# RWKV scan: odd pairs of heads change sides of the partitions at each step of the triangular inverse

## What is computed

```
def step(S, inp):
    r_t, w_t, k_t, v_t, a_t, b_t = inp
    sa = einsum('bhvk,bhk->bhv', S, a_t)
    S = S * w_t[:, :, None, :] + sa[..., None] * b_t[:, :, None, :] + v_t[..., None] * k_t[:, :, None, :]
    return S, einsum('bhvk,bhk->bhv', S, r_t)
```

## Time and profile before

| what | us |
|---|---|
| median of 3 runs | 1949.92 |
| runs | 1946.99 to 1952.98 |
| the profiled execution | 1955.08 |
| its span | 1953.3 |
| TensorE busy in the span | 1862.2 |
| VectorE busy | 1290.7 |
| ScalarE busy | 1026.4 |
| scan, first L2753 to the first matmul after it (L413) | 152.06 |

### The profile page before, as it was taken

How to read it: one execution, slowest core, us unless ns; L and a number is a source line. 1 busy time by engine, 2 the same in 40 slices (tenths; PEclk the granted TensorE clock), 3 DMA queues, 4 the chain that set the end, 5 groups by cost and what they waited for, 6 DMA issues and landing times.

```text
span 1953.3 us, 46364 instructions
## 1 busy us (share of the span) xinstructions
PE 1862.2 (95%) x17956; PEld 1782.7 (91%) x17956; DVE 1290.7 (66%) x2627; ACT 1026.4 (53%) x2027; POOL 45.2 (2%) x38
## 2 busy tenths in 40 slices
PE   6999989999988999999999999999989978999998
PEld 6999989999988999989899999999976878899998
DVE  5778676778675665586566664766476755557764
ACT  5556646556645555555465554655445733245553
POOL 2110001110000000000000000000000000000000
PEclk9999999999998999999999999999989979989999
DMA  7444555445553555532235555555541500035654
GB/s 259 153 150 154 158 168 164 147 148 158 152 183 108 182 173 173 167 105 89 64 111 160 174 173 179 162 172 172 182 164 56 152 12 4 4 92 179 185 183 127
DMA packets 75675, 278.05 MB, mean 142 GB/s; under 512 B 8336, under 2 KB 9744, under 8 KB 75024
## 3 DMA queue, kind: packets, MB, share of 16 engines
q1 hardware_dynamic: 75536, 276.04, 45.5%
HBM read 274.96 MB, written 1.05 MB: 141 GB/s over the span
## 4 chain that ended last, share of the span: by engine, by line
PE 81%; DVE 10%; ACT 5%; issue 2%; DMA 1%; DVEq 0%; SPq 0%; ACTq 0%
PE psum L413 23%; PE psum L415 22%; PE psum L414 22%; DVE weights_low L378 4%; ACT weights_high L370 2%; PE psum L2835 1%; PE psum L2818 1%; PE psum L2832 1%; PE psum L1900 1%; PE psum L2776 1%; PE psum L2535 1%; PE psum L2753 1%; PE psum L718 1%; PE psum L1145 1%; PE psum L739 1%
## 5 line engine op out<-in xcount | busy, mean ns | idle before, releaser
L378 DVE TENSOR_TENSOR weights_low<-weight_ring,weights_high 128x512 fp32r<-128x512 f32 x988 | 669.7, 697 | 482.5 <-ACT weights_high L370 472.8
L370 ACT ACTIVATE weights_high<-weight_ring 128x512 fp32r<-128x512 f32 x988 | 608.4, 628 | 552.6 <-PE psum L415 547.4
L413 PE MATMUL psum<-ffn_normed_high,weights_high 128*128 128x272 f32 (+1 forms) x1408 | 407.4, 289 | 7.9 <-DVE ffn_normed_low L646 5.2
L415 PE MATMUL psum<-ffn_normed_high,weights_low 128*128 128x272 f32 (+1 forms) x1408 | 405.7, 288 | 0.0
L414 PE MATMUL psum<-ffn_normed_low,weights_high 128*128 128x272 f32 (+1 forms) x1408 | 404.4, 287 | 0.0
L413 PE MATMUL psum<-first_normed_high,weights_high 128*128 128x256 f32 x1024 | 297.8, 291 | 12.5 <-DVE first_normed_low L432 7.1
L414 PE MATMUL psum<-first_normed_low,weights_high 128*128 128x256 f32 x1024 | 287.1, 280 | 0.0
L415 PE MATMUL psum<-first_normed_high,weights_low 128*128 128x256 f32 x1024 | 287.0, 280 | 0.0
L413 PEld LDWEIGHTS psum<-ffn_normed_high,weights_high 128*128 128x128 f32 x1408 | 266.5, 189 | 11.0 <-issue 10.8
L415 PEld LDWEIGHTS psum<-ffn_normed_high,weights_low 128*128 128x128 f32 x1408 | 266.5, 189 | 0.0
L414 PEld LDWEIGHTS psum<-ffn_normed_low,weights_high 128*128 128x128 f32 x1408 | 266.4, 189 | 0.1
(11 more groups left out here) (450 smaller groups left out, 3193.7 us busy)
## 6 DMA issues: line engine op xcount, KB each, us to landing
weight_ring<-weights_in SPq DMA_DIRECT2D x508, 512.0 KB, 3.6
arena<-first_in SPq DMA_DIRECT2D x1, 2176.0 KB, 8.2
consts<-const_in SPq DMA_DIRECT2D x1, 1895.0 KB, 12.4
arena<-vec_in SPq DMA_DIRECT2D x1, 1536.0 KB, 9.3
arena<-vec_in SPq DMA_DIRECT2D x1, 1152.0 KB, 5.9
residual<-x_in SPq DMA_DIRECT2D x2, 544.0 KB, 6.9
out<-normed SPq DMA_DIRECT2D x4, 256.0 KB, 2.4
vectors<-vec_in SPq DMA_DIRECT2D x1, 255.0 KB, 4.2
```

The lines of the kernel that those rows point to most:

```text
L370: nc.scalar.activation(WH[:, n % SPLIT, half], W[:, n % RING, half], ACT.Copy).then_inc(weights_high, 1)
L378: nc.vector.tensor_tensor(WL[:, n % SPLIT, half], W[:, n % RING, half], WH[:, n % SPLIT, half].bitcast(F32), ALU.subtract).then_inc(weight ...
L413: nc.tensor.matmul(psum, WH[:, s, cols], high, start=start, stop=False)
L415: return nc.tensor.matmul(psum, WL[:, s, cols], high, start=False, stop=stop)
```

## The change

Pairs with odd `k` change sides. In a product that reads a head's rows in `half(o)`, an odd pair's result now goes to the other half (`lane(k, o)`), and in the next product it reads from there and comes back. So `pe_ax`, `pe_xax`'s X, `pe_ur`'s second part and `pe_u` use all four quarters of the array: even pairs the two on the diagonal, odd pairs the other two. `RX`'s products always end in `half(o)`; `RY` and `RXT` of odd pairs lie in `lane(k, o)`. The transposed part therefore stays on the diagonal for all pairs, in the order 0, 1, 1, 0.

`SLOT` puts even pairs in the first four slots of 64 columns and odd pairs in the last four, and `X_PS` (columns 256 to 767 of PSUM) and `U_PS` straddle two banks, so that the two quarters that write the same partitions write different banks. The turns get bank 3, transposed parts bank 2, y bank 7, state and sums bank 6.

The flip also makes the odd pairs' matrix on the other side (`CROSS`, 8 more products, in the turns' bank), and so waits for ScalarE's copy of the turned values. In `dve_first` the masks of even pairs are half as wide, those of odd pairs are read from `CROSS` behind the flip, and the `xt` subtraction moves behind the flip too. Turns 1 and 2 are no longer groups of their own: their products are laid between those of the transposed parts of rounds 2 and 3 (for chunk 1: of rounds 1 and 2 of chunk 0). `pe_ur` waits earlier for the state and also for `y_taken`, `pe_y_sums` for the state.

```
+        def lane(k, o):
+            return half(o ^ (k % 2))
...
+        def turn_tile(c, j, k, o):
+            into = const("centre_half" if j == 2 else "ident_half")
+            return nc.tensor.matmul(PS[lies(j, o), TURN_BANK, SLOT[k] * TC:(SLOT[k] + 1) * TC], (BT, KT, V_)[j][half(o), k, wide(c)],
+                                    into[half(o)], start=True, stop=True)
...
         def pe_flip(pe, c):
             pe.wait_ge(rs["gram_taken"], 2 * c + 2)
-            for k, o in heads():
-                mm = nc.tensor.matmul(spot(0, k, o), GR[c % 3][half(o), o, k, 0], const("ident_half")[half(o)], start=True, stop=True)
+            pe.wait_ge(rs["turned_taken"], 3 * c + 3)
+            flip = lambda k, o: nc.tensor.matmul(X_PS[half(o), SLOT[k]], GR[c % 3][half(o), o, k, 0], const("ident_half")[half(o)],
+                                                 start=True, stop=True)
+            for k in range(1, KC, 2):
+                for o in range(2):
+                    nc.tensor.matmul(CROSS[lane(k, o), k // 2], const("ident_half")[half(o)], GR[c % 3][half(o), o, k, 0], start=True, stop=True)
+                for o in range(2):
+                    flip(k - 1, o)
+            for k in range(1, KC, 2):
+                for o in range(2):
+                    mm = flip(k, o)
...
             for o in range(2):
-                dve_chain.later(nc.vector.tensor_tensor(xt[half(o)], GR[c % 3][half(o), o, :, 0],
-                                                        const("pairs_half")[half(o)].unsqueeze(1).broadcast_to([TC, KC, TC]), ALU.mult))
+                dve_chain.later(nc.vector.tensor_tensor(xt[half(o), 0:KC // 2], GR[c % 3][half(o), o, 0:KC:2, 0], pairs[half(o)], ALU.mult))
+            dve.wait_ge(rs["ax_ready"], rounds_before(c) + c + 1)
+            dve_chain.later(nc.vector.tensor_tensor(RX, X_PS, const("partners_half")[:, 0:TC].unsqueeze(1).broadcast_to([P, KC, TC]), ALU.mult))
+            dve_chain.later(nc.vector.tensor_tensor(xt[:, KC // 2:KC], CROSS, pairs, ALU.mult))
             dve_chain.settle()
+            dve_chain.later(nc.vector.tensor_tensor(RX, eye, RX, ALU.subtract))
             dve_chain.later(nc.vector.tensor_tensor(xt, eye, xt, ALU.subtract))
...
         def pe_ax(pe, c, i):
             pe.wait_ge(rs["x_new"], rounds_before(c) + i + 1)
             for k, o in heads():
-                mm = nc.tensor.matmul(spot(0, k, o), GR[c % 3][half(o), o, k, 0], RX[half(o), k], start=True, stop=True)
+                mm = nc.tensor.matmul(X_PS[lane(k, o), SLOT[k]], GR[c % 3][half(o), o, k, 0], RX[half(o), SLOT[k]], start=True, stop=True)
...
-                    mm = nc.tensor.matmul(spot(0, k, o), RXT[c % 2][half(o), k], RY[half(o), k], start=True, stop=True)
+                    mm = nc.tensor.matmul(X_PS[half(o), SLOT[k]], xt(k, o), y(k, o), start=True, stop=True)
                 mm.then_inc(rs["xax_ready"], 1)
...
+            if turn:
+                pe.wait_ge(rs["turned_taken"], 3 * turn[0] + turn[1])
+            for k in range(KC):
+                for o in range(2):
+                    mm = nc.tensor.matmul(PS[lane(k, o), XT_BANK, SLOT[k] * TC:(SLOT[k] + 1) * TC], y(k, o), xt(k, o), start=True, stop=True)
+                if k == KC - 1:
+                    mm.then_inc(rs["xaxt_ready"], 1)
+                if turn:
+                    for o in range(2):
+                        mm = turn_tile(*turn, k, o)
...
         def pe_u(pe, c):
             pe.wait_ge(rs["xt_new"], rounds_before(c + 1))
             pe.wait_ge(rs["ur_taken"], c + 1)
             for k, o in heads():
-                mm = nc.tensor.matmul(spot(2, k, o), RXT[c % 2][half(o), k], UR[half(o), k], start=True, stop=True)
+                mm = nc.tensor.matmul(U_PS[half(o), SLOT[k]], RXT[c % 2][lane(k, o), SLOT[k]], UR[lane(k, o), SLOT[k]], start=True, stop=True)
```

More of the change, by code:

```diff
@@ L2775, in pe_turn @@
             for k, o in heads():
-                mm = nc.tensor.matmul(PS[lies(j, o), 6, k * TC:(k + 1) * TC], (BT, KT, V_)[j][half(o), k, wide(c)],
-                                      into[half(o)], start=True, stop=True)
+                mm = turn_tile(c, j, k, o)
             mm.then_inc(rs["turned"], 1)
@@ L2784, in act_turn @@
                 rows = slice(at, at + (R_WIDTHS[c] if j == 2 else TC))
-                step = nc.scalar.activation((KEYS, KEYS, VALUES)[j][c % 3][rows, o], halves(6, KC)[rows], ACT.Copy)
+                step = nc.scalar.activation((KEYS, KEYS, VALUES)[j][c % 3][rows, o], halves(TURN_BANK, KC)[rows], ACT.Copy)
             step.then_inc(rs["turned_taken"], 1)
@@ L2823, in dve_ax, with pe_xax @@
             mask = const("partners_half")[:, (1 + i) * TC:(2 + i) * TC].unsqueeze(1).broadcast_to([P, KC, TC])
-            nc.vector.tensor_tensor(RY, halves(0, KC), mask, ALU.mult).then_inc(rs["ax_taken"], 1)
-        def pe_xax(pe, c, i):
+            nc.vector.tensor_tensor(RY, X_PS, mask, ALU.mult).then_inc(rs["ax_taken"], 1)
+        def pe_xax(pe, c, i, turn=None):
             pe.wait_ge(rs["ax_taken"], rounds_before(c) + i + 1)
@@ L2829, in pe_xax @@
                 pe.wait_ge(rs["xt_new"], rounds_before(c) + i)
+            xt = lambda k, o: RXT[c % 2][lane(k, o), SLOT[k]]
+            y = lambda k, o: RY[lane(k, o), SLOT[k]]
             if i < R_ROUNDS[c] - 1:
                 for k, o in heads():
-                    mm = nc.tensor.matmul(spot(0, k, o), RXT[c % 2][half(o), k], RY[half(o), k], start=True, stop=True)
+                    mm = nc.tensor.matmul(X_PS[half(o), SLOT[k]], xt(k, o), y(k, o), start=True, stop=True)
                 mm.then_inc(rs["xax_ready"], 1)
-            for k, o in heads():
-                mm = nc.tensor.matmul(spot(1, k, o), RY[half(o), k], RXT[c % 2][half(o), k], start=True, stop=True)
-            mm.then_inc(rs["xaxt_ready"], 1)
+            if turn:
[8 more added lines that the diff above has]
+                        mm = turn_tile(*turn, k, o)
+            if turn:
+                mm.then_inc(rs["turned"], 1)
         def dve_xax(dve, c, i):
@@ L3002, in act_rwkv_scan @@
                 for o in range(2):
-                    step = nc.scalar.activation(VALUES[c % 3][half(o), o], halves(2, KC)[half(o)], ACT.Copy, scale=-1.0)
+                    step = nc.scalar.activation(VALUES[c % 3][half(o), o], U_PS[half(o)], ACT.Copy, scale=-1.0)
                 step.then_inc(rs["u_taken"], 1)
@@ L3057, in dve_rwkv_scan @@
                     if c:
-                        dve_chain(nc.vector.tensor_tensor(new, old, halves(2, KC), ALU.add))
-                    nc.vector.tensor_tensor(new, new if c else halves(2, KC), EC[:, :, c:c + 1].broadcast_to([P, KC, 64]), ALU.mult)\
+                        dve_chain(nc.vector.tensor_tensor(new, old, halves(UR_BANK, KC), ALU.add))
+                    nc.vector.tensor_tensor(new, new if c else halves(UR_BANK, KC), EC[:, :, c:c + 1].broadcast_to([P, KC, 64]), ALU.mult)\
                         .then_inc(rs["state_ready"], 1)
```

55 lines of the change are left out of this document (29 added, 26 removed).

## The result

| | before | after |
|---|---|---|
| median us | 1952.74 (5 runs) | 1937.78 (5 runs) |
| lowest to highest | 1946.99 to 1953.63 | 1937.33 to 1940.6 |
| span of the profiled execution | 1953.3 | 1936.0 |

The ratio is 0.9933, with a 95% interval of 0.9919 to 0.9946: 13 us less, between 10.5 and 15.8 (the two medians lie 15.0 apart). The forecast was 20 us less, to 1930; the forecast's own range ended at 1937. The median before, from five runs now, lies 2.8 us above the one that the forecast started from.

The account below looks back on a forecast made before the run. TensorE's products were taken as the bound, VectorE's latency where nothing fills in. Savings of 5.2, 10.7, 3.9 and 0.9 us less 0.5 at the start gave 20.2 us, from median 1949.92 to 1930; range 1923 to 1937.

Parts of the forecast that it names:

- the group's price: Inverse's 16-product groups in four quarters: 0.47 us unbroken and 0.68 after a wait, from 0.93 and 1.15.
- twelve starts: Earlier trace, 1646.42 to 1646.59: twelve matmul starts within 0.17 us, 15 ns each, taken as four quarters running at once.
- the walk through a step: Chunk 1 or 2, timed group by group: first product to last transposed part 19.12 us, 5.05 saved.
- rival C: Scan: longer TensorE gaps drop the granted clock to 1.2 GHz; about 1970 us if throughout; chance 0.06.
- A: Four-quarter groups gain nothing, held by program order or instruction feeding: +0 to +5 us, about 1953; chance 0.09.
- the half-clock stretch: Chunk 0's step: 3.4 us at half the granted clock, some 1.7 of its 28.46 us, assumed to stay.
- end: Chunk 4: two groups on the path, L2860 and L2867, at 0.47 us each, 0.9 us saved.
- B: Partial feeding: starts between 15 and 29 ns apart, 0.6 to 0.8 us per group, about 1940 us; chance 0.09.
- the start: Before the scan's steps: the flip's later starts less what chunk 0's three rounds save, net +0.5 us.
- The two waits of the flip: Flip waits for ScalarE's copy of turned values: about 2.1 us for chunk 0, 1.0 for chunk 1.
- what chunk 0's rounds give back: Three rounds at the start save 2.6 us: three products, two X of 0.47, and two merged turns.
- the merged turns: Full step: two turns sharing the array with transposed parts save some 0.75 us net each.

Follow-up runs that it names:

- the wide burst: Kernel after plus test bursts; this one repeats 128 products with 256 columns streamed: 13.7 us in four quarters, 27.4 in two, first start to last.
- the one-side run: Kernel after with odd pairs not changing sides, so the inverse's products use two quarters again; ratio 0.9998 against the kernel before.
- the run with the flip's own bank: Kernel after with the flip's extra products in a separate bank, without waiting for ScalarE's copy of the turned values; ratio 0.9906 against the kernel before.
- the run with the turns apart: Kernel after with turns 1 and 2 as groups of their own in their old places; ratio 0.9911 against the kernel before.

## Why the prediction was right, and where it was off

**Right: the group's price.** 0.68 us whole and 0.47 unbroken were forecast, 0.69 and 0.47 measured. The evidence of the earlier trace rows, twelve starts, bore the claim that the four quarters run independently; the wide burst shows it for 14 us. The Trainium skill's rule of starts in strict program order ("TensorE: Matmul & The Clock Gate", Part 3) does not hold in the earlier trace rows, nor after the change: a product's first starts (L2845, 1658.16) lie ahead of a turn's last two (L2787, 1658.20).

**Right: the walk through a step.** From step 1's first product to its last transposed part I had 19.12 us; the chain has 1624.55 to 1644.10, 19.55, with a pause of 0.36 in it. The wait for the mask in round 3 was forecast at 0.8 and is 0.80 at 1664.81 (step 2). From the last transposed part to the next first product: 4.78 forecast, 4.90 measured (1644.10 to 1649.00). The clock stayed at 1.00 in all steps, so rival C did not come; nor did A, as the one-side run shows what A would have been (0.9998).

**Off: the sum, 20.2 against 16.2 in the scan's windows** (15.0 between the medians, 13 by the ratio). Step by step, saved in us, forecast and measured: step 0 5.2 and 5.9 (the half-clock stretch that I had left in both was gone, which alone is 1.7; it is gone in the one-side run too, so the quarters did not remove it, and whether other executions before had it no trace shows: that part may be luck); step 1 5.4 and 5.1; step 2 5.4 and 3.5; step 3 3.9 and 2.5; end 0.9 and 1.2; start +0.5 and +2.0.

The step that failed is the one from twelve starts to whole groups: the 15 ns of a sample "fed from a queue that had filled" went into the sum for every four-quarter group, and the coming in of instructions, which I named in rivals A and B, has no term in it. Nor does it work as B had it: it does not stretch each start but stops the row after 128 matmuls, until a packet has come. The pauses within the groups of the steps, start to start, are 0.68 and 0.73 us in step 0, 0.58 in step 1, 0.52, 0.47, 0.46 and 0.79 in step 2, 0.86 and 0.28 in step 3: 5.4 us, some 4.9 of them more than the usual step between two starts. That is the size of the missing term, if all of it lies on the path. By this estimate step 0 would be 21.3 without its pauses, step 1 23.6, step 2 23.7 and step 3 20.5, near the 21.6, 23.9, 23.9 and 20.1 of the walk. The chance of 0.09 for B was too low, and its time, about 1940, is nearer to the result than my 1930. Two of the recorded figures don't follow from their own terms: the range's end is 1949.9 - 15 + 3 = 1938, not 1937, and C's 1970 adds its 35 us to the profiled execution's 1934.9, where the median's 1930 gives 1965.

**Off: the start.** The two waits of the flip cost 2.8 us in the view of waits and 2.6 by experiment; I had 3.1. What I overrated is what chunk 0's rounds give back: without the flip's wait the start is 31.4 against 32.07, so 0.6 and not 2.6 are left for it after the eight extra products of two flips. I had not walked these rounds, and TensorE stands still in them at two places where it had not before: 0.83 us for VectorE's mask ahead of X (1592.16) and 0.97 ahead of the transposed part with turn 2 (1595.23), put down to ScalarE's copy of turn 1. Both are there, as long, in the run with the flip's own bank. Together, 1.8 us, they are nearly all of the missing 2; one of the pauses (1595.93 to 1596.33) lies there too.

**Off: the merged turns**, one term in the steps: some 1.5 us per step in my sum (two of 0.75), 0.65 (1.3 in two steps) by the run with the turns apart. The pauses account for the difference: less the usual step they come to 2.5 us in steps 1 and 2 of the kernel after and to 0.3 with the turns apart, and without them the two would lie some 3.6 us apart (an estimate), near the 3 of my sum.

## What to carry to other kernels

Before giving small products more quarters of the array, count the instructions per microsecond that it would then eat: here 128 matmuls with their 128 weight loads came in no faster than every 3.5 to 3.8 us, 27 to 29 ns per matmul, which two quarters with 64 columns of float32 use up already. Short groups between waits do gain, because instructions that came in during the waits are used up at 15 ns; long rows don't. So what pays next is the same columns in fewer instructions (one product with 256 columns in place of four), and a borrowed PSUM bank is worth a look for the wait that comes with it.

## What the runs showed of the hardware that I had not expected

- TensorE's instructions come in by packets of 16 KB, one for 128 matmuls and 128 loads (12 packets more for 1536 matmuls more). In a row of four-quarter products one such packet lasts 1.88 us, TensorE is idle for 1.66 us, and the next row starts 3.75 us after the last did, twice, and once 3.48.
- TensorE goes on 1.24 to 1.56 us after such a packet's end (42 of 42 pauses), and the next packet starts 1.05 to 1.27 us later still (39 of 42). The packets themselves took 0.88 to 1.35 us in the six rows above.
- With 256 columns streamed, 256 matmuls take 13.7 us in four quarters and 27.4 in two, from first start to last. The least step between starts that the page "TensorE: Matmul & The Clock Gate" of the Trainium skill gives, 25 ns, does not bound matmuls in different quarters: 15 ns over 128 in a row here.
- Whether a pause shows is a matter of where it falls: sixteen products more per step made one step 0.9 us longer and the next 0.7 shorter, and with 12 matmuls fewer in each flip three pauses were left of eight. What decides when a packet is asked for, and so why not two come ahead of need, stays open. So does whether it matters that quarters that write the same partitions write different banks: no run puts them into one.
